# Weight tiles moved by 16 to 96 bytes within a partition, a different amount in each stage

## What is computed

```python
# first network, even layer: 512 latent and 256 context tokens
p = h @ ev_w_in                       # projections
x = x + gate * (mix @ ev_w_out)       # output
x = x + gate * (square(relu(h @ mlp_w1[0])) @ mlp_w2[0])
# first network, odd layer: 512 latent tokens, context only in some projections
p = h @ od_w_in
x = x + gate * (mix @ od_w_out)
x = x + gate * (square(relu(h @ mlp_w1[1])) @ mlp_w2[1])
# second network, twice
z = h @ w_in
y = sigmoid(g_a) * (mla(z) @ w_proj_a) + sigmoid(g_b) * (hgrn(z) @ w_proj_b)
x = x + y @ w_out
x = x + (silu(h @ w_gate) * (h @ w_up)) @ w_down
```

## The kernel before

| stage | 512 columns | 256 columns | distance before, mod 128 | after: high | after: low |
|---|---|---|---|---|---|
| even projections | 528 | 384 | 0 | 32 | 16 |
| even output | 192 | 192 | 0 | 32 | 32 |
| even MLP | 1536 | 1536 | 0 | 64 | 48 |
| odd projections | 696 | 216 | 64 | 0 | 0 |
| odd output | 192 | 0 | 0 | 96 | 80 |
| odd MLP | 1536 | 0 | 0 | 96 | 96 |
| second layers, both | 5760 | 0 | 0 | 32 | 16 |

## Time and profile before

### The profile page before, as it was taken

One profiled execution on the slowest core, in us unless ns is written; L12 is line 12 of the kernel. 1 busy time (PEld: TensorE's weight loads), 2 busy tenths in 40 slices (PEclk: granted clock), 3 DMA queues, 4 the chain that ended last, 5 costly groups with the idle time before them and its releaser, 6 DMA issues. The chain is left out here.

```text
span 3934.4 us, 45661 instructions
## 1 busy us (share of the span) xinstructions
PE 3645.1 (93%) x18494; PEld 2932.7 (75%) x18494; DVE 2035.1 (52%) x3169; ACT 864.5 (22%) x1690; POOL 1369.6 (35%) x599
## 2 busy tenths in 40 slices
PE   6898988999989999968999899799999898899998
PEld 3684567888877889857888566688888576788887
DVE  5797643224446457673233367864243377853342
ACT  3213512110011233301100344422000344421001
POOL 2331043225554200005455222235455222245454
PEclk9898989999999999989999899999999999999999
DMA  5443312221113100112322232123332222223322
GB/s 171 150 150 134 129 43 75 60 64 59 61 53 91 51 1 1 51 45 73 98 94 91 61 81 53 50 67 100 97 92 80 82 61 54 52 78 96 97 91 80
DMA packets 400349, 306.78 MB, mean 78 GB/s; under 512 B 11228, under 2 KB 367782, under 8 KB 399559
## 3 DMA queue, kind: packets, MB, share of 16 engines
q1 hardware_dynamic: 398040, 303.37, 25.5%
q10 hardware_dynamic: 2095, 0.44, 0.1%
HBM read 297.48 MB, written 6.29 MB: 77 GB/s over the span
## 5 line engine op out<-in xcount | busy, mean ns | idle before, releaser
L450 POOL TENSOR_TENSOR low<-raw,high 128x1024 fp32r<-128x1024 f32 (+1 forms) x437 | 1049.5, 2402 | 2090.4 <-DVE high L356 2090.4
L519 PE MATMUL scores<-high 128*128 128x512 f32 (+1 forms) x1944 | 741.5, 381 | 72.0 <-DVE low L704 32.4
L519 PE MATMUL scores<-low,high 128*128 128x512 f32 (+1 forms) x1944 | 727.1, 374 | 0.0
L519 PE MATMUL scores<-high,low 128*128 128x512 f32 (+1 forms) x1944 | 726.3, 374 | 0.0
L356 DVE CAST high<-raw 128x1024 fp32r<-128x1024 f32 (+1 forms) x437 | 397.5, 910 | 499.6 <-PE scores L519 257.7
L519 PE MATMUL bank<-high 128*128 128x512 f32 (+1 forms) x1480 | 541.5, 366 | 0.2
L519 PE MATMUL bank<-low,high 128*128 128x512 f32 (+1 forms) x1480 | 538.8, 364 | 0.0
L519 PE MATMUL bank<-high,low 128*128 128x512 f32 (+1 forms) x1480 | 538.1, 364 | 0.0
L519 PEld LDWEIGHTS scores<-high 128*128 128x128 f32 x1944 | 375.5, 193 | 154.2 <-POOL low L450 53.9
L519 PEld LDWEIGHTS scores<-high,low 128*128 128x128 f32 x1944 | 374.6, 193 | 65.5
L519 PEld LDWEIGHTS scores<-low,high 128*128 128x128 f32 x1944 | 376.2, 194 | 61.7 <-issue 1.0
(11 more groups left out here) (632 smaller groups left out, 5260.2 us busy)
## 6 DMA issues: line engine op xcount, KB each, us to landing
raw<-in_mlp_w SPq DMA_DIRECT2D x128, 512.0 KB, 3.9
raw<-in_w_in SPq DMA_DIRECT2D x76, 512.0 KB, 3.9
ring<-in_ada_w SPq DMA_DIRECT2D x32, 1024.0 KB, 7.1
raw<-in_w_gate SPq DMA_DIRECT2D x44, 512.0 KB, 3.8
raw<-in_w_up SPq DMA_DIRECT2D x44, 512.0 KB, 3.8
raw<-in_w_down SPq DMA_DIRECT2D x40, 512.0 KB, 3.4
mix<-in_ada_w SPq DMA_DIRECT2D x16, 1024.0 KB, 6.3
raw<-in_od_w_in SPq DMA_DIRECT2D x29, 512.0 KB, 3.9
```

Source lines behind the costliest of these rows:

```text
L450: pool.tensor_tensor(tile(low, u), tile(raw, u), tile(high, u).bitcast(F32), ALU.subtract)\
L519: mm = pe.matmul(out(p), stationary, moving, start=(k0 + k == 0 and i == 0), stop=(k0 + k == job.kc - 1 and i == len(pairs) - 1))
```

## The change

`products` gets a number `skew`, in floats. The buffer `low` is longer by it, and the tiles of `low` begin that much further on. `high` lies behind `low` and so begins further on too, by the same amount rounded up to 32 bytes. `raw`, the activations and everything allocated ahead of `low` stay where they are. The instructions of all engines, their order and their waits are the same.

```diff
 def products(nc, m, jobs, ring_tiles=RING, ...
-             before=None, loads=(), sides=(), banks=8, sums=None, settled=False):
+             before=None, loads=(), sides=(), banks=8, sums=None, settled=False, skew=0):
...
-        raw, low, high = held.enter_context(buffers(nc, raw=[P, R, 1024], low=([P, RH, 1024], F32R),
+        raw, low, high = held.enter_context(buffers(nc, raw=[P, R, 1024], low=([P, RH * 1024 + skew], F32R),
                                                     high=([P, RH, 1024], F32R)))
+        low = low[:, skew:].rearrange("p (r n) -> p r n", r=RH)
```

More of the change, by code:

```diff
@@ L1755, in squared_relu_mlp @@
                              lead=6 if own_room else 1, room_after=None if own_room else 0)],
-                 ring_tiles=3, before=before, sides=sides, sums=SquareSums(m, x, toks))
+                 ring_tiles=3, before=before, sides=sides, sums=SquareSums(m, x, toks), skew=24 if own_room else 12)
 class Rows:
@@ L1909, in even_mixer @@
                                  beside=convolve, signals=("convolved",), with_signals=convolution_signals, before=before,
-                                 ring_tiles=3, banks=6, sides=[copies, Modulation(
+                                 ring_tiles=3, banks=6, skew=4, sides=[copies, Modulation(
                                      m, A, [(0, n) for n in range(4, 12)],
@@ L1932, in even_output @@
                              room=halves)],
-                 ring_tiles=3, sides=[Gain(gain, mods, small.norm_g[:, 1, :], 4)], sums=SquareSums(m, x, toks))
+                 ring_tiles=3, sides=[Gain(gain, mods, small.norm_g[:, 1, :], 4)], sums=SquareSums(m, x, toks), skew=8)
 def even_mlp(nc, m, A, x, mods, later, small, gain):
@@ L2750, in odd_layer @@
                                  residual(x, shift(2))((LAT,)), "vector", room=halves)],
-                     sides=[Gain(gain, mods, small.norm_g[:, 3, :], 4)], sums=SquareSums(m, x, (LAT,)))
+                     sides=[Gain(gain, mods, small.norm_g[:, 3, :], 4)], sums=SquareSums(m, x, (LAT,)), skew=20)
     squared_relu_mlp(nc, m, x, A["mlp_w1"][1, :, :], A["mlp_w2"][1, :, :], (LAT,), scale, shift(3), shift(5))
@@ L2873, in odd_projections @@
         beside=convolve, signals=("convolved",), with_signals=with_signals, before=before,
-        ring_tiles=3, banks=7, sides=[delta])
+        ring_tiles=3, banks=7, skew=16, sides=[delta])
 MH, MQK, MNOPE, MV = 8, 96, 64, 64
@@ L3924, in layer_products @@
             written_by=15, room=halves, room_after=13, lead=6)],
-        before=before, ring_tiles=3, settled=True, sides=[constants, prep, attention, forget, levels, gates, states, norm], sums=SquareSums(m, x, toks))
+        before=before, ring_tiles=3, settled=True, skew=4, sides=[constants, prep, attention, forget, levels, gates, states, norm], sums=SquareSums(m, x, toks))
 def program(nc, A, out):
```

## The result

The changed kernel takes 3981.0 us, median of two runs (3976.83 and 3985.17), beside 3940.62 before: a ratio of 1.0101, 95% interval 1.0072 to 1.013. That is 40 us or 1% slower, twice the 19 us forecast, and inside the stated range of 3915 to 4015. The profiled execution has a span of 3983.0 us, 48.6 more than before; its own time is 3985.17, the upper of the two runs, so the spans differ by more than the medians.

The account below looks back on a forecast made before the run. The prediction took PE's matmul count and start-to-start pace as the bound. Stage terms summed to +19.1 us on the profiled 3934.4, giving 3953.5; 6.2 for the runs' median made 3959.7, say 3960, range 3915 to 4015.

Parts of the forecast that it names:

- the likeliest case: The forecast itself, all stages: matmuls priced by weight-activation distance, 3960 us in all; chance 0.42.
- the flank rival: All matmul stages: a step just past distance 0 costs nearly a whole 128-byte turn; +71 us, 4012; chance 0.15.
- the straight line: PE's matmuls: 6.67 ns x distance / 64, loss at 512 columns, gain at 256; second layers +16.0 us.
- Passing the sum on whole: PE's matmul streams: no slack there, so all +19.1 us was added to the kernel's time.
- nothing: All matmul stages: distance has no price, the odd projections differ by something else; 3941 us; chance 0.16.
- The zero for POOL and DVE: POOL's subtraction and the cast: no effect taken, with up to 4 us and 2 us thought possible.
- The row taken as a bound: L1614, multiplying tensors at different offsets: 1398 ns against the subtraction's 1288 at 512 elements, some 110 ns either way.
- The even stages near zero: Even projections +0.4 us, even MLP +9.4 - 9.4 = 0, even output 0.
- the bounds of that step: 512-column matmul pace at unseen distances: 226.7 to 235 ns; with 256-column gains, -19 to +81 us overall.
- 128 counts as 0, 96 as 32, 80 as 48: Distances fold back at a 128-byte turn: odd MLP +5.1, odd output +0.8, odd projections -3.2 us.
- coincidence only: Matmuls: only distance 0 at 256 columns and 64 at 512 cost; elsewhere lowest paces; 3923 us; chance 0.18.
- Relief: Matmuls: distances not near 0 or 64 free a collision of weight load and moving operand; -173 us, 3768; chance 0.09.

Follow-up runs that it names:

- experiment 1: The changed kernel with raw moved along with low and high, so the three are at one offset again; 3973.33 us, ratio 1.0096.
- experiment 2: The kernel before with a 64-byte gap ahead of the program's first tensor, every distance kept; 3939.14 us, ratio 1.0007.
- experiment 3: The changed kernel with low and high back at their old distances to the activations and raw alone displaced behind them; 3935.24 us, ratio 0.9989.
- experiment 4: The changed kernel with raw, low and high moved together by other amounts, one distance per stage (second layers 64, odd projections 256 bytes); 3975.31 us, ratio 1.0095.
- experiment 9: Kernel of experiment 8 with the even stages' context activations in their own tensors, 64 bytes nearer the weights than the latents; 3925.86 us, ratio 0.9971.
- experiment 5: Kernel before, low and high displaced, raw fixed: fine distances in several stages, second layers high alone 64, odd MLP low weights and low activations 64; 3961.97 us, ratio 1.0064.
- experiment 8: The kernel before with the odd projections' low and high moved on 192 bytes, to distance 256; 3932.51 us beside 3936.16, ratio 0.9987.
- experiment 6: Kernel before, low and high displaced, raw fixed: distances 4, 8, 240, 248, second layers 192, odd MLP low weights alone 64; 3955.64 us, ratio 1.0042.
- experiment 10: Kernel of experiment 8 with raw put behind low and high and 8 bytes further on in every stage; 3913.38 us, ratio 0.9945.

## Why the prediction was right, and where it was not

The cause and its sign were right, the sizes were not: 40 us in place of 19. The stated range took that in, but the likeliest case's own range, 3945 to 3980, missed the median by 1 us. The range held because it was also drawn for the flank rival, not because the straight line was right.

What held:
- The bound. The time follows PE's pace; 5760 steps of the second layers by 232.4 less 227.2 ns are 30.0 us, and those stages grew by 30.6. Passing the sum on whole was right.
- The cause. The distance between weights and activations sets the pace: experiments 1 to 4 leave no room for the place alone, for `raw`, or for the rival "nothing", and in experiment 9 one weight slice runs at two distances side by side.
- The zero for POOL and DVE. 2427 ns against 2423, and experiments 1 and 3. It held because all amounts of the change are multiples of 16 bytes (2490 ns at 16 in experiment 5, beside 2488 before). The row taken as a bound, an unlike pair 110 ns slower, did not bound it: at 4 or 8 bytes the subtraction gets 400 ns faster, and that shows in the time.
- The even stages near zero: 0.5, 0.8 and 0.9 us against 0.4, 0 and 0. The sizes behind it were off: in the even MLP the two widths moved by +3.2 and -3.2 ns, not by 6.11, and cancelled all the same. The base there was off too, since 226.7 is the last of three paces of the earlier trace rows and the stage's mean is 228.1.

What failed:
- "A straight line from one to the other and back". Between 0 and 64 there is no slope; the price is there from the first four bytes. The second layers were put at 2.78 ns and paid 5.2, +30.6 us in place of +16.0. It was drawn because "none lies between"; the bounds of that step (226.7 to 235) did hold the truth for this stage.
- "128 counts as 0, 96 as 32, 80 as 48". The turn is 256 bytes. The odd MLP at 96 paid 7.6 ns and not 3.33 (+11.4 us in place of +5.1), the odd output at 96 and 80 paid 8.7 and not 3.89 (+2.8 in place of +0.8, of which 192 x 8.7 ns are 1.7; the granted clock of that stretch was 0.93 in place of 0.96), and the odd projections at 128 did not fall to 226.7 but stayed at 232.7 (+0.7 in place of -3.2). The prediction had named that as a sign of a wrong turn or another cause, and experiments 4 and 8 show the turn. The prediction called both ends of that last term rows; but 128 had no row, only 0 had. The trace of before held distances 0 and 64 alone (modulo 256), which fit a turn of 128 and of 256 alike.

These five terms, -3.2 + 0.8 + 5.1 + 16.0 and the even stages' 0.4, made 19.1; the measured ones make 47.7.

The rivals: "nothing" and "coincidence only" fall with the second layers at 232.4. "Relief" falls with the table: no distance brings a stage's mean under 226.7 at 512 columns. "The other flank" was nearer than the forecast in kind, since a step just past 0 does cost most of the price at once; but its 237 ns was not reached, and its turn of 128 was wrong as well.

The page "SBUF — State Buffer" of the Trainium skill, section "Who interferes with whom", gives PE two independent read ports and lets it wait on nobody. Experiment 2 against 1 shows that the same instructions at the same granted clock take 227.2 or 233.3 ns by the relative place of PE's own two operands alone. The trace does not agree with ports that are independent in every respect, and the measurement decides; what ties the two operands together is not shown.

## What to carry to other kernels

Where matmuls with fresh weights run back to back, the addresses of both operands within a partition are a tuning knob: compare the pace of like instructions between stages, tabulate the operands' distance modulo 256 bytes, and try 0 first for wide matmuls. When a cost has only two known points, don't interpolate a price over addresses, and don't take the shortest period that fits: price the unseen distances at the worse known point. A zero effect measured at offsets that share a factor (here 16 bytes) says nothing on the others.

## What was not expected of the hardware

- PE's pace depends on where its two operands lie to each other in a partition, with a turn of 256 bytes: four bytes of displacement take 512 columns from 226.7 to over 232 ns, while 192 bytes take them only to 229; at 256 columns 64 bytes gain up to 6.7 ns.
- At one distance a stream can run at more than one steady pace (113.4 and 117.7 ns at 256 columns and distance 64, experiments 1 and 9).
- POOL's subtraction of 1024 columns takes 2400 ns with `raw` and the halves at one offset modulo 16 bytes, 2010 or 2004 with 4 or 8 bytes between them (even MLP of experiments 5 and 6), and 2430 with 12 (odd projections of experiment 5).
- The DVE instruction that lowers the activations takes 0.75 us with POOL idle; started during POOL's subtraction it ended only after it, in 2.44 us beside 2.39 and 2.05 beside 2.00 (experiments 8 and 10).
